# A two-layer encoder step on one core: norm rows spread over the partitions by TensorE instead of by broadcast loads

## What is computed

```
xp = layernorm(x_prompt, ln0_g, ln0_b)
xs = layernorm(x_sample, ln0_g, ln0_b)
for i in range(DEPTH):
    ...
    proj = x @ lp['w_in']
    ...
    x = layernorm(DN_ALPHA * x + merged @ lp['w_out'], lp['ln1_g'], lp['ln1_b'])
    moe_out = hier_moe(x, lp['w_rg'], lp['w_re'], lp['w1'], lp['w3'], lp['w2'])
    ple_term = jax.nn.sigmoid(x @ lp['w_ple_gate']) * (ple @ lp['w_ple'])
    x = layernorm(DN_ALPHA * x + moe_out + ple_term, lp['ln2_g'], lp['ln2_b'])
```

## Time and profile before

| | us |
|---|---|
| median of 3 runs | 1637.58 |
| lowest and highest | 1634.08, 1637.85 |
| the profiled execution | 1633.66 |
| its span, first to last instruction | 1631.9 |
| TensorE busy | 1345.5 (82%) |
| VectorE busy | 452.2 (28%) |
| ScalarE busy | 268.5 (16%) |
| chain that ended last: TensorE, DMA | 56%, 33% |
| moved by DMA | 493.17 MB, 302 GB/s over the span |

### The profile page before, as it was taken

One profiled execution on the slowest core, in us unless ns is written; L12 is line 12 of the kernel. 1 busy time (PEld: TensorE's weight loads), 2 busy tenths in 40 slices (PEclk: granted clock), 3 DMA queues, 4 the chain that ended last, 5 costly groups with the idle time before them and its releaser, 6 DMA issues.

```text
span 1631.9 us, 21415 instructions
## 1 busy us (share of the span) xinstructions
PE 1345.5 (82%) x9148; PEld 677.9 (42%) x9149; DVE 452.2 (28%) x996; ACT 268.5 (16%) x665; POOL 51.3 (3%) x97
## 2 busy tenths in 40 slices
PE   6999999999977666766599999999999657667663
PEld 4556665553523222322155656645544213223311
DVE  3241563451211011100244426625421011011004
ACT  2442322120100000000045323220201000000000
POOL 1300000000000000000021000000000000000000
PEclk9999999999989879888799999999999888888876
DMA  9402414779999999999962053149799999999992
GB/s 333 153 1 104 162 52 150 301 294 424 426 427 426 426 427 426 427 427 427 401 198 79 2 183 132 47 166 392 309 426 426 427 427 426 427 427 426 427 425 103
DMA packets 100180, 493.17 MB, mean 302 GB/s; under 512 B 9552, under 2 KB 15472, under 8 KB 52336
## 3 DMA queue, kind: packets, MB, share of 16 engines
q1 hardware_dynamic: 94912, 478.17, 71.9%
q0 software_dynamic: 5168, 13.55, 2.7%
HBM read 488.78 MB, written 2.89 MB: 301 GB/s over the span
## 4 chain that ended last, share of the span: by engine, by line
PE 56%; DMA 33%; SPq 5%; DVE 4%; issue 1%; ACT 1%; POOL 0%; DVEq 0%; ACTq 0%
PE bank L926 54%; DMA arena<-in_w_e_down 11%; DMA arena<-in_w_e_up 8%; DMA ring<-in_w_e_gate 5%; SPq L734 5%; DMA ring<-in_w_e_down 4%; DMA ring<-in_w_e_up 3%; PE bank L963 2%; DMA arena<-in_w_e_gate 2%; DMA ring<-in_w_in 1%; DVE arena L2229 0%; DVE small L1810 0%; DVE x_sb L1832 0%; DVE arena L1827 0%; DVE arena L2297 0%
## 5 line engine op out<-in xcount | busy, mean ns | idle before, releaser
L926 PE MATMUL bank<-arena 128*32 128x512 f32 (+9 forms) x2744 | 518.1, 539 | 150.0 <-DMA arena<-in_w_e_gate 34.6
L926 PE MATMUL bank<-ring,xT 128*32 128x128 f32 (+5 forms) x2688 | 436.6, 377 | 4.2 <-DVE xT L1845 2.4
L926 PE MATMUL bank<-ring,arena 128*32 128x512 f32 (+4 forms) x1760 | 413.6, 596 | 2.7 <-ACT arena L1777 2.7
L926 PEld LDWEIGHTS bank<-arena 128*32 128x32 f32 (+4 forms) x2744 | 200.0, 142 | 375.5 <-issue 363.6
L926 PEld LDWEIGHTS bank<-ring,xT 128*32 128x32 f32 (+1 forms) x2688 | 216.8, 139 | 194.5 <-issue 184.1
L926 PE MATMUL bank<-cst,arena 128*32 128x512 f32 (+2 forms) x224 | 122.4, 689 | 51.4 <-DMA arena<-in_w_e_up 32.7
L926 PEld LDWEIGHTS bank<-ring,arena 128*32 128x32 f32 (+1 forms) x1760 | 118.8, 132 | 79.3 <-issue 69.4
L926 PE MATMUL bank<-arena,x_sb 128*128 128x128 f32 (+1 forms) x768 | 99.7, 282 | 1.4 <-DVE arena L2136 0.8
L926 PEld LDWEIGHTS bank<-arena,x_sb 128*128 128x128 f32 (+1 forms) x768 | 90.5, 190 | 19.4 <-issue 12.7
L2286 DVE TENSOR_TENSOR arena<-arena,bank 128x512 f32<-128x512 f32 x16 | 11.0, 688 | 273.2 <-PE bank L926 273.2
L926 PE MATMUL bank<-xT,arena 128*32 128x512 f32 x112 | 58.6, 673 | 31.9 <-DMA arena<-in_w_e_down 20.4
(11 more groups left out here) (218 smaller groups left out, 845.8 us busy)
## 6 DMA issues: line engine op xcount, KB each, us to landing
arena<-in_w_e_gate SPq DMA_DIRECT2D x68, 1024.0 KB, 26.1
arena<-in_w_e_up SPq DMA_DIRECT2D x62, 1024.0 KB, 26.2
arena<-in_w_e_down SPq DMA_DIRECT2D x58, 1024.0 KB, 26.4
ring<-in_w_e_up SPq DMA_DIRECT2D x48, 1024.0 KB, 26.6
ring<-in_w_e_gate SPq DMA_DIRECT2D x44, 1024.0 KB, 26.5
ring<-in_w_e_down SPq DMA_DIRECT2D x42, 1024.0 KB, 26.5
ring<-in_w_in SPq DMA_DIRECT2D x32, 1024.0 KB, 9.5
lb<-in_w_e_gate SPq DMA_DIRECT2D x14, 1024.0 KB, 25.8
```

The costliest lines, as they stand in the source:

```text
L926: return pe.matmul(out, lhsT, rhs, start=first, stop=last, skip_group_check=True)
```

## The change

The rows of the first norm and of each layer's last norm are no longer broadcast by DMA. Each pair of rows is loaded as it is, onto four partitions of a tile `rows` (4 x 512: g's halves on partitions 0 and 1, b's on 2 and 3). For r = 0 to 3 TensorE multiplies: stationary is column r of the identity's first four rows, repeated 128 times (4 x 128), moving is `rows`, so that every one of the 128 output partitions holds row r. ScalarE copies each bank to its quarter of `lnw`. The rows of the middle norm are still broadcast.

At the start the identity and the two small loads are issued ahead of x; the spread is TensorE's first work. In each layer POOL issues the small loads when the last ple job is done (`rows` lies where pT lay), and the spread stands in quad 1 behind `hT`, in banks 7 and 0 by turns. VectorE's first norm of a kind waits for the four copies instead of for the load.

```diff
--- before.py
+++ after.py
@@ -237,6 +237,8 @@
     if g:
         j += tokens
     j += [(("hT",), 4)]
+    if g == 1:
+        j += [(("row", r), (7, 0)[r % 2]) for r in range(4)]
     j += [(("Y", 0), 5), (("Y", 1), 6)] + plain(0, 0, 7, 0) + plain(1, 1, 1, 2) + plain(1, 2, 3, 4) + combine
     if not g:
         j += tokens
@@ -258,6 +260,8 @@
             n += 1
             uses[b] += 1
 
+        for r in range(4):
+            enter(("row", r), r)
         for layer in range(DEPTH):
             for k, job in enumerate(JOBS):
                 enter((layer,) + job, k % BANKS)
@@ -507,6 +511,7 @@
         sel = carve(2304, 3, 128)
         selw = carve(2688, 3, 128)
         pT = carve(3072, 2, T)
+        rows = carve(3072, 512)
         selT = carve(3648, T)
         rl = carve(3648, 3, 64)
         route = carve(3840, 3, 32)
@@ -572,6 +577,7 @@
         consts_in = sem("consts_in")
         ident_in = sem("ident_in")
         ln0_in = sem("ln0_in")
+        ln2_in = sem("ln2_in")
         x_in = sem("x_in")
         lnw_in = sem("lnw_in")
         rows_in = sem("rows_in")
@@ -751,12 +757,12 @@
                 elif BEFORE[n] is not None:
                     wait_used(BEFORE[n])
 
+            sp.dma_start(ident, consts[:, C_ID:C_ID + P]).then_inc(ident_in, 16)
+            for k, row in enumerate((ln0_g, ln0_b)):
+                sp.dma_start(rows[2 * k:2 * k + 2, :], row.rearrange("(j n) -> j n", j=2)).then_inc(ln0_in, 16)
             for t in range(3):
                 src = x_prompt[0, T0[t]:T0[t] + P, :] if t < 2 else x_sample[0]
                 sp.dma_start(x[0:NT[t], t, :], src).then_inc(x_in, 16)
-            sp.dma_start(lnw[:, 0, :], ln0_g.partition_broadcast(P)).then_inc(ln0_in, 16)
-            sp.dma_start(lnw[:, 1, :], ln0_b.partition_broadcast(P)).then_inc(ln0_in, 16)
-            sp.dma_start(ident, consts[:, C_ID:C_ID + P]).then_inc(ident_in, 16)
             for layer in range(DEPTH):
                 win = w_in[layer].rearrange("(p c) n -> p c n", c=8)
                 experts = dict(eg=w_e_gate[layer].rearrange("e (p h c) n -> e p h (c n)", p=P, h=2),
@@ -897,8 +903,9 @@
                 pool.dma_start(pT[:, :, SEQ:T], p_sample[layer]).then_inc(ple_in, 16)
                 pool.wait_ge(mg_out, 6 * layer + 3)
                 load_ln(1 + 2 * layer, ln1_g[layer], ln1_b[layer])
-                job_done(pool, (layer, "moe", 0, "U"))
-                load_ln(2 + 2 * layer, ln2_g[layer], ln2_b[layer])
+                job_done(pool, (layer, "pl", 1, 2))
+                for k, row in enumerate((ln2_g[layer], ln2_b[layer])):
+                    pool.dma_start(rows[2 * k:2 * k + 2, :], row.rearrange("(j n) -> j n", j=2)).then_inc(ln2_in, 16)
                 pool.wait_ge(stored, 16 * 8 * (layer + 1))
             for t in range(3):
                 pool.wait_ge(ln_out, 3 * 2 * DEPTH + t + 1)
@@ -969,6 +976,16 @@
             pe.sem_inc(more_matmuls, 1)
             pe.wait_ge(ident_in, 16)
             pe.wait_ge(eps_set, 1)
+
+            def spread_rows(keys):
+
+                for r in range(4):
+                    b = open_bank(keys[r])
+                    one_row = ident[0:4, r:r + 1].broadcast_to([4, P])
+                    done(mm(b[:, :], one_row, rows[0:4, :], True, True))
+
+            pe.wait_ge(ln0_in, 32)
+            spread_rows([("row", r) for r in range(4)])
             for layer in range(DEPTH):
                 def turn_tile(name, norms, t):
 
@@ -1431,6 +1448,9 @@
                     for c in range(4):
                         ins = pe.transpose(b[:, c * P:(c + 1) * P], hid[:, c:DE:4], ident)
                     done(ins)
+                    if g == 1:
+                        pe.wait_ge(ln2_in, 32 * (layer + 1))
+                        spread_rows([key("row", r) for r in range(4)])
                     job_read(pe, key("hT"))
                     if g == QUADS - 1:
                         for job in COMBINE_JOBS + [("Y", 0), ("Y", 1), ("XT", 0), ("XT", 1)]:
@@ -1515,6 +1535,14 @@
             act.reg_mov(turn, 0)
             logs_and_exps()
             act.wait_ge(eps_set, 1)
+
+            def keep_rows(keys):
+
+                for r in range(4):
+                    job_done(act, keys[r])
+                    emptied(act.copy(lnw[:, r // 2, 512 * (r % 2):512 * (r % 2) + 512], bank(keys[r])[:, :]), keys[r])
+
+            keep_rows([("row", r) for r in range(4)])
             norm_and_turn(0, 0)
             for layer in range(DEPTH):
 
@@ -1775,6 +1803,8 @@
                     key = (layer, "moe", g, "hT")
                     job_done(act, key)
                     emptied(act.copy(hidT[:, :, :], bank(key)[:, :].rearrange("p (c t) -> p c t", c=4)), key)
+                    if g == 1:
+                        keep_rows([(layer, "moe", g, "row", r) for r in range(4)])
                     if g == QUADS - 1:
                         further_passes(act, layer, turn, more)
                         logs_and_exps()
@@ -1820,7 +1850,11 @@
                 n, at = NT[t], ln_place(k, t)
                 dve.bn_aggr(mvs[0:n, 2 * t:2 * t + 2], ln_st[0:n, :]).then_inc(ln_var, 1)
                 if at == 3 * k + 1:
-                    dve.wait_ge(*((lnw_in, 32 * k) if k else (ln0_in, 32)))
+                    if k % 2:
+                        dve.wait_ge(lnw_in, 16 * (k + 1))
+                    else:
+                        for r in range(4):
+                            job_read(dve, (k // 2 - 1, "moe", 1, "row", r) if k else ("row", r))
                 dve.wait_ge(ln_var, at)
                 parts = [slice(0, 512), slice(512, 1024)] if first_half else [slice(0, 1024)]
                 for cols in parts:
```

## The result

| | before | changed |
|---|---|---|
| median, 8 runs each on one chip, us | 1636.78 | 1640.70 |
| lowest and highest | 1633.80, 1637.85 | 1638.08, 1643.04 |
| the profiled execution | 1633.66 | 1642.57 |
| its span | 1631.9 | 1640.8 |
| TensorE busy | 1345.5 | 1364.0 |

The ratio is 1.0026, with a 95% interval of 1.0016 to 1.0036: 3.9 us slower where 7.2 us less had been forecast. That is just within the 0.3% counted as no change, on the other side of zero, and outside the range of 1625.5 to 1636. So the changed kernel is slower by 0.1 to 0.3%; the first comparison is clear of zero, the second is not, and neither leaves room for the gain that was forecast.

A forecast was written before the change was run, and what follows sets the result against it. TensorE was taken to bound the dense stages and full transfers the expert stages. The start's -2.3 us and the experts' -4.9 us sum to -7.2, taking the median from 1637.58 to 1630.4 us, range 1625.5 to 1636.

The forecast's parts named there:

- x: it landed 7.65 us; later by 0 to 1.3 us, since POOL's loads and x share the engines: Start: x was to land at 8.4 us, the middle of that range, letting VectorE normalize at 10.1 instead of 12.44.
- small loads hold x back: Rival at the start: three small loads paid one after another land x at 13.65 us; -2.0 us in all, chance 0.12.
- The w_in chain: Start: with 1.049 MB less in front, the w_in pieces land at 14.15 us instead of 16.8.
- Four products at the slow pace, 0.83 us each: Start: the spread's products done by 7.8 us and the last row copy by 8.5 us.
- The forecast of 14.5 us for the first product: Start: x's norm and w_in both allow the first w_in product at about 14.5 us, a gain of 2.3 us.
- 2.46 us of all DMA engines, per layer: Expert stages: 1.049 MB fewer broadcast bytes at 427 GB/s, saved in full in each of two layers, -4.9 us.
- The thin queue: Rival in the expert stages: layer 1's queue empties or broadcasts filled spare time; half of 4.9 us goes, 1632.8, chance 0.14.
- windows below 420 GB/s: Sign of being wrong: DMA windows under 420 GB/s between 1185 and 1250 us, in layer 1.
- Nothing in it is an excess of DMA time that hides: Expert stages: the removed broadcasts' DMA time counts in full, -2.46 us for each of two layers.
- 0 on the path: Quad 1: the spread makes TensorE 1.7 us later, hidden by a 2.49 us down-weight wait, 0.8 us to spare.
- Scatter of several us from code that now lies elsewhere: Remainder: scatter from moved code, TensorE standing 7.8 us at the last quad for nothing visible; chance 0.04.
- The "slower" rival: Rival in quad 1: late norm rows stop TensorE ahead of the down products; 90 us landing gives 1643.3, chance 0.04.

The follow-up runs named there:

- the second: The changed kernel unedited, run again against the kernel before on another chip: 1640.03 us, ratio 1.0008 [0.9997, 1.0020].
- with POOL held: The changed kernel with POOL's first five loads held back until x has landed: 1637.16 us, ratio 1.0003 to the kernel before.
- experts alone: The kernel before with its old start, but the experts' norm rows spread by TensorE in quad 1: 1633.58 us, ratio 0.9984.
- start alone: The kernel before with only the new start, the experts' norm rows still broadcast: 1639.40 us, ratio 1.0018.
- before with 54 more: The kernel before plus 54 empty semaphore increments on TensorE at the start, before 14.8 us: 1642.37 us, ratio 1.0036.
- twin: The kernel before run against itself without any edit: 1637.99 against 1636.53 us, ratio 1.0009.
- in quad 2: The kernel before with its old start, the experts' norm rows spread in quad 2 between gate and up products: 1634.04 us, ratio 0.9983.
- before with 202 more: The kernel before plus 202 empty semaphore increments on TensorE in quads 3 to 6 of layer 0: 1636.23 against 1638.11 us, ratio 0.9985.
- changed with 202 more: The changed kernel plus 202 empty TensorE increments in quads 3 to 6 of layer 0: 1633.38 us, ratio 0.9983 to the kernel before.
- start mended: Changed kernel with x first, identity and rows on ScalarE's queue, split norm wait, spread in quad 2, 202 increments: 1632.93 us, 0.9970 of the kernel before.
- all together: Changed kernel with POOL waiting for x, split norm wait, spread in quad 2, 202 increments: 1627.62 against 1638.11 us for the kernel before, ratio 0.9940.

## Why the prediction was wrong, point by point

**The start: x.** The step that failed reads "x: it landed 7.65 us; later by 0 to 1.3 us, since POOL's loads and x share the engines". It landed at 12.3 us. The landing took 9.6 us from the issue instead of 6.0, because the 1.1 us by which x is issued later let POOL's loads in ahead of it, and from 4 to 6 us the engines then move 178 GB/s instead of 397. In a sum by bytes POOL's 0.7 MB stand before x or behind it at equal cost; in the trace x pays for them alone. The rival "small loads hold x back" gave the right symptom and the wrong mechanism: with POOL held and the small loads in place, x was on time. Instead of -2.3 us the start cost +1.3. The w_in chain did run as forecast: with POOL held, the first product starts with no wait for w_in.

**The start: the spread.** "Four products at the slow pace, 0.83 us each" was the second wrong price. The trace has x8 instructions for four products, 7.16 us in all: 1.79 us a product. The row "16 in 7.03" is of 8 products too. In this kernel a float32 product of this kind is two instructions: 0.88 us a product in that row, and 1.71 us from one copy of the spread to the next at the start. (The granted clock reads 1.00 from 3 to 10 us all the same; the pace there is half of the full one.) So VectorE could not have normalized at 10.1 us with everything else right, but at 11.1 as with POOL held back. The forecast of 14.5 us for the first product would have been 15.2, unless VectorE starts with half of the rows; that version reaches 14.12.

**The experts: bytes.** "2.46 us of all DMA engines, per layer" came to about 1.3. The thin queue, one of the rivals, exists: of the signs for being wrong, "windows below 420 GB/s" came true. The windows at the start of layer 1's expert stage, before and changed:

```profile
1224.00:1240.00 16.00, 16.00 (x143) 7.70 (x145) 2.06 (x7) 2.86 (x4) 0.00 (x0) 1.00 1.01 425
```

```profile
1224.00:1240.00 16.00, 15.70 (x126) 9.02 (x128) 3.81 (x7) 2.27 (x3) 0.00 (x0) 1.00 1.01 407
1240.00:1260.00 20.00, 20.00 (x149) 10.08 (x145) 2.75 (x8) 4.11 (x7) 0.00 (x0) 0.98 1.00 421
```

18 GB/s less for 16 us and 5 less for 20 us (426 before) are 0.39 MB, or 0.9 us of the queue: of 2.46 us 1.5 would be left. But across all thirteen traces the thin queue does not explain the missing half. From 1180 to 1260 us the five kernels with the broadcasts move 425 or 426 GB/s. Of the eight without them five are thin, 420 to 422, and three are not, 425 or 426 (those with the 202 increments). The time from the hidden tile of quad 0 to that of quad 7 in this layer is

| kernels | rate, GB/s | us |
|---|---|---|
| five with the broadcasts | 425, 426 | 398.0 to 398.3 |
| five without, thin | 420 to 422 | 395.8 to 397.4 |
| three without, full | 425, 426 | 397.9 to 398.0 |

The thin ones gained more, not less. On average the bytes gave 0.9 us here and 1.8 us in layer 0 (398.1 to 400.4 with the broadcasts, 395.3 to 398.1 without), 2.7 us of the 4.9, as the run of the experts alone has it. Why it is not more stays open: the step that failed is "Nothing in it is an excess of DMA time that hides", and only its size is measured.

**The experts: the spread in quad 1.** The places were misread: what the earlier trace rows call quad 1 is quad 2. The hidden tile of quad 1 is turned 28 us ahead of the first long DMA wait, and its down products wait for no transfer, as TensorE's timeline of the kernel before has it:

```profile
447.76 0.75 PE L1432 MATMUL bank<-cst,arena 128*128 128x128 f32 x4
449.19 3.64 PE L926 MATMUL bank<-ring,arena 128*32 128x512 f32 x32 [0.68 <-ACT arena L1777]
```

Changed kernel, with ScalarE's first copy:

```profile
452.22 0.75 PE L1449 MATMUL bank<-cst,arena 128*128 128x128 f32 x4
...
452.89 3.77 PE L933 MATMUL bank<-arena,cst 4*128 4x512 f32 x8
...
454.05 0.58 ACT L1543 COPY lnw<-bank 128x512 f32<-128x512 f32 x1 [0.47 <-PE bank L933]
...
456.60 3.92 PE L933 MATMUL bank<-ring,arena 128*32 128x512 f32 x20
```

From hidden tile to down products it is 4.4 us where it was 1.4, so the spread costs 3.0 us rather than 1.7. It costs 1.7 us more behind it, since the down products follow at the lower clock (windows of the changed kernel):

```profile
455.00:457.00 2.00, 2.00 (x8) 0.45 (x10) 0.00 (x0) 1.38 (x3) 0.00 (x0) 1.00 0.98 414
457.00:459.00 2.00, 2.00 (x16) 0.55 (x12) 0.00 (x0) 0.29 (x1) 0.00 (x0) 0.56 1.04 438
459.00:461.00 2.00, 2.00 (x16) 0.53 (x12) 0.00 (x0) 0.00 (x0) 0.00 (x0) 0.59 0.99 418
461.00:463.00 2.00, 2.00 (x24) 0.54 (x20) 0.00 (x0) 0.00 (x0) 0.00 (x0) 1.00 1.02 422
```

In the kernel before it is 1.00 from 447 to 457 us. Still "0 on the path" came out right, for another reason than the one given. All of it is taken up by the waits of quad 2, as the run with the spread there shows.

**The remainder.** "Scatter of several us from code that now lies elsewhere", with a chance of 0.04, was the largest single cause. The stand at the last quad went from 7.65 to 12.00 us in layer 1, and layer 0 got a second one of 0.58. With the down products behind them, the two layers take 4.7 us longer (41.1 instead of 36.5), nearly all of it in layer 1. Putting the kernel before into the same place made it 5.5 us slower; moving the changed kernel's code on took off 7.0 us (0.9983 against 1.0026) by the first comparison of the changed kernel and 4.1 (against 1.0008) by the second. The "slower" rival named, a late row pair in quad 1, did not occur: no wait for `ln2_in` stands in the trace.

**The sum** of what was measured: +1.3 (start) - 2.6 (experts; the two marks give 2.5) + 4.7 (the two jumps with what follows them) = +3.4 us, against +3.9 [2.6, 5.9] in the first comparison of medians and +1.3 [-0.5, 3.3] in the second. Shown by experiment are the sign and the place of each term. They do not add as measured alone: start alone (+2.9) and experts alone (-2.6) make +0.3, since each puts the code elsewhere, and only both together put it in the dear place. A check on the third term is that the two kernels which differ from the one before by increments alone, +5.9 and -2.5 us by their ratios, come to +0.5 and -0.2 us once their longer or shorter stretches behind the jumps (+5.4, -2.3) are taken off.

## What to carry to other kernels

A load moved back by one microsecond can lose several if it falls behind another queue's loads, so read which queue's transfers would then be ahead of it, and do not count them at the full rate. Before hiding work behind a wait, make sure that the wait belongs to the iteration in which the work stands, and take the price of an operation from a row whose instructions per operation you have counted. Where an engine jumps over code and stands for nothing that the profile shows, treat any edit of its instruction count as a change of its own: measure it alone, and compare kernels in which the target of the jump lies alike; the same number of added instructions does not make it so.

## What the hardware showed that was not expected

**A jump's price depends on where its target lies.** In the last quad TensorE reads that no further passes are needed and jumps over their code. In 13 traces with two layers each, the stand behind it took 7.6 to 7.9 us in 22 of 26 places. The other four are all in layer 1: 12.00 and 12.01 us in the changed kernel and its repeat, 13.05 us where POOL waits for x and in the kernel before with 54 more. The table gives the time from the last hidden tile to the end of the 64 down products, which holds the stand, any second one and the pace behind them. The target is counted in the program, from the start of TensorE's instructions, each product and each turned piece taken as four; it serves to compare places only.

| target in layer 1 | kernels | us |
|---|---|---|
| 20,822 | before, twin | 18.2, 18.1 |
| 20,842 | start alone | 19.1 |
| 20,856 | experts alone; in quad 2 | 20.0; 18.5 |
| 20,876 | changed, repeat, POOL waits, before with 54 more | 22.8, 22.8, 22.7, 22.6 |
| 21,024 | before with 202 more | 16.9 |
| 21,078 | changed with 202 more; start mended; all together | 18.1; 18.4; 17.5 |

The four at 20,876 agree within 0.2 us, though their stands read 12.0 and 13.05, and cost 4.5 us. Two kernels at one place can also differ by 1.5 us (20,856), so the place is not all. In layer 0 no target lies so badly: 19.2 us at 10,372 (54 more), 17.1 to 18.5 in the others. There the 202 increments moved the changed kernel's target by 239 from its place in the kernel before and not by a multiple of 256, as the expectation has it; that holds in layer 1 alone.

Instructions come by DMA themselves, as the page of the changed kernel shows, 16.4 KB a packet:

```profile
q8 instruction: 78, 1.28, 0.3%
```

The likely reading is that the target's block has to be fetched through a queue full of weights, and that in the bad place the next block is needed at once. This is argued: no run here took the weights away. The Trainium skill (Runtime: NRT & Kernel Launch, section Instruction fetch mechanics) says that blocks of 16 KiB are prefetched in sequence only and that a taken branch out of the window stalls until its page is fetched. The packets of 16.4 KB and the stand of 7.6 us and more behind every one of these jumps agree with it. Which offsets are good, and why the down products behind the jump also took 1 us less in the kernel before with the code moved, stays open.

**Loads from POOL can hold back a large load of SyncE issued after them.** POOL issues five, three of them broadcasts, 0.7 MB in all. With them let in first, the engines moved 178 GB/s from 4 to 6 us, at a busy share of 0.79; held back, 397 at 1.01; with x ahead of them, 324. The last part of x, 128 KB, took 9.6, 5.0 and 6.0 us to landing.

**The spread is followed by the lower clock.** Four products with four partitions of weights each, and as many columns as any others: behind them in quad 1 the granted clock was 0.56 and 0.59 for 4 us in the changed kernel. In the run of the experts alone it averages 0.83 from 440 to 460 us, where the kernel before has 1.00. With the spread in quad 2 the up products that follow come 0.85 us apart instead of 0.43 for 3 us. What TensorE did before each fall was this spread, without a pause of note: in the changed kernel its instructions start 0.42 to 0.51 us apart (455.22 and 455.65 us, for example), where 0.43 is the pace without a wait. So the few partitions are the likelier cause than the waits for ScalarE's copies, but no run here spreads with more of them.
